# Gated recurrence: cumulated decays made two rounds ahead, and their logarithm moved to the begin of a round

## The chip, the cores and the metric

One NeuronCore of a Trainium2 chip runs the kernel; the other cores are idle. The metric is the time of one execution on the device in microseconds (us), lower is better. It is taken over several executions of the same compiled program, without the profiler.

## The reference, cut to what matters

The kernel computes two blocks, one behind the other, on 256 positions of 1024 channels, in fp32. The first block has a mixer with two branches (a gated linear recurrence, HGRN2, and a Mamba-2 recurrence) and a gated feed-forward net. The second has retention and a convolution as mixer, and 16 experts, each 1024 x 2048 twice and 2048 x 1024 once. The change touches only the HGRN2 branch, which has 8 heads of 128 channels and 272 positions (16 learned ones ahead of the 256):

```python
f = lb + (1.0 - lb) * jax.nn.sigmoid(f_pre)      # lb: one value for each channel
k = 1.0 - f
log_f = jnp.log(f)
bcum = jnp.cumsum(gc, axis=2)                    # gc: log_f in chunks
blast = bcum[:, :, -1]
q_dec = qc * jnp.exp(bcum)
k_inv = kc * jnp.exp(-bcum)
k_end = kc * jnp.exp(blast[:, :, None] - bcum)
...
o = o * lax.rsqrt(jnp.mean(o * o, axis=-1, keepdims=True) + EPS)
return (o * norm_w * jax.nn.silu(g))
```

## The kernel before

All engines run programs written out by hand, and they meet only at semaphores; an engine works through its own program strictly in the written order. Channels lie on the 128 partitions and positions along the free dimension, so one head of HGRN2 is one tile of 128 x 272.

The first block's input projection has 52 column tiles of 128 channels, j = 0 to 51. TensorE (PE) computes tile j (L872) and ScalarE (ACT) evicts it from one of three PSUM banks, with the activation that the column needs (evict, L1254). PE may open tile j only when tile j-3 has been evicted. The work of the recurrences is hung between these tiles: each engine's loop over j first does its share of the recurrences, then its share of the tile. From j = 32 on, head h of HGRN2 is worked on in round h, the three tiles j = 32+3h, 33+3h and 34+3h. What a round does, engine by engine:

- PE: in the first third `hg_turn(h)` (L784). It waits for `hg_staged` (the decayed queries and keys are ready), transposes values and keys (L793, L795), computes four levels of scores (L802), waits for `hg_v`, does one small score product (L804), waits for `hg_ke` and computes the state updates (L808). In the second third `hg_out(h)` (L815 to L818), which waits for `hg_masked`. In the last third `hg_mean(h)` (L826).
- VectorE (DVE): in the first third `hg_values(h)` (copies of the transposed values, L1845, L1846), `hg_mask(h)` (L1853, L1855), `hg_states(h)` (L1859, L1860), then `hg_cumulate(h+1)`; in the second third `hg_gate(h)` (L1867), `hg_finish(h-1)` (L1872) and `hg_decay(h+1)` (L1835 to L1840), whose end raises `hg_staged`.
- ACT: in the first third `hg_keys(h)` (L1373), `hg_log_mean(h-1)` (L1365), `hg_log(h+1)` (L1351), `hg_inverse(h-1)` (L1369); then it waits for the head's output, squares it (L1390) and does `hg_exps(h+1)` (L1356 to L1358); only then it evicts the tile.

`hg_cumulate(h)` is the step around which the change turns. It forms the gate f from the sigmoid in one DVE instruction (L1817, waited for), tells ACT (`hg_f`), forms k = 1 - f (L1819), waits for ACT's logarithm (`hg_log`), does four scans over chunks of 16, 32, 64 and 128 positions (L1822) and four differences (L1826), and raises `hg_b`:

```python
st.link(ts(hg_f, proj[:, h + TF_, :], oml[:, h:h + 1], lb[:, h:h + 1], ALU.mult, ALU.add))
dve.nop().then_inc(ev("hg_f"), 1)
st(ts(hg_k, hg_f, -1.0, 1.0, ALU.mult, ALU.add))
dve.wait_ge(ev("hg_log"), h + 1)
for l in range(4):
    st(dve.tensor_tensor_scan(hg_B[:, b, l, :], reset[:, l, :], hg_lf, 0.0, ALU.mult, ALU.add))
```

`hg_exps(h)` waits for `hg_b`, and `hg_decay(h)` for the exponentials (`hg_exp`). hg_B, hg_D and hg_K0 have two buffers, by h modulo 2; the logarithm hg_lf and the key factor hg_k have one each. Head 0 is prepared ahead of the rounds, at j = 30: behind the last output of Mamba-2 (`m2_out`, L1794) DVE clears two tiles (L1925, L1926) and calls `hg_cumulate(0)` and `hg_decay(0)`. Between the rounds stand two more pieces: the gating of Mamba-2's outputs on DVE (`m2_gate`, L1800, at j = 48 and behind the loop), whose squares ACT takes at j = 49 (L1400), and the modulation of the second block (L1668, L1717 on PE and DVE's L1672) in round 0.

The weights are streamed from HBM by one queue, SP's. Each transfer waits until PE has counted the slot of the ring free (`units_used`). In the second block's experts the same ring takes 2 MB units.

Of the kernel before, what the change touches and what calls it, by code (L numbers as in the profile page):

```python
# [19 lines left out]
ACT = mybir.ActivationFunctionType  # L20
ALU = mybir.AluOpType
# [11 lines left out]
HEADS = 8  # L33
# [15 lines left out]
TQ, TF_, TI, TG, TZ, TX, TBM, TCM = 0, 8, 16, 24, 32, 40, 48, 50  # L49
# [101 lines left out]
def build(nc, a, out):  # L151
    with ExitStack() as ctx:
# [5 lines left out]
        def ev(name):  # L158

            if name not in sems:  # L160
                sems[name] = ctx.enter_context(nc.semaphore("s_" + name))
            return sems[name]
# [30 lines left out]
        small = sb("small", [P, 256])  # L193
# [38 lines left out]
        proj = A.take(NPROJ, T)  # L232
# [24 lines left out]
        hg_S = A.take(2, P)  # L257
        hg_inv = A.take(1, T)[:, 0]

        hg_f, hg_k, hg_lf, hg_sq = (proj[:, TBM + i, :] for i in range(4))  # L260

        A = Arena(x_at)
        m2_t = A.take(2, T)
# [984 lines left out]
        def _(act):  # L1248
            st = Steps(act, ev("act_steps"))
# [97 lines left out]
                    act.activation(buf, buf, ACT.Exp).then_inc(ev("m2_seg_exp"), 1)  # L1347

            def hg_log(h):
                act.wait_ge(ev("hg_f"), h + 1)  # L1350
                act.activation(hg_lf, hg_f, ACT.Ln).then_inc(ev("hg_log"), 1)  # L1351

            def hg_exps(h):
                b = h % 2
                act.wait_ge(ev("hg_b"), h + 1)
                st(act.activation(hg_K0[:, b], hg_B[:, b, 0, :], ACT.Exp, scale=-1.0))  # L1356
                st.link(act.activation(hg_D[:, b], hg_D[:, b], ACT.Exp))
                act.activation(hg_B[:, b], hg_B[:, b], ACT.Exp).then_inc(ev("hg_exp"), 1)  # L1358
# [16 lines left out]
            def hgrn(j):  # L1375
                h = (j - 32) // 3
                if j < 32 or h >= HEADS:
                    return
                if (j - 32) % 3 == 0:
                    hg_keys(h)  # L1380
                    if h:
                        hg_log_mean(h - 1)
                    if h + 1 < HEADS:
                        hg_log(h + 1)
                    if h:
                        hg_inverse(h - 1)
                    act.wait_ge(ev("hg_out"), h + 1)
                    if h:
                        act.wait_ge(ev("hg_mean"), h)
                    act.activation(hg_sq, ps[:, 6, 0:T], ACT.Square).then_inc(ev("hg_squared"), 1)  # L1390
                    if h + 1 < HEADS:
                        hg_exps(h + 1)
                if (j - 32) % 3 == 2 and h == HEADS - 1:
                    hg_log_mean(h)
                    hg_inverse(h)
# [58 lines left out]
            for i in range(FT):  # L1454
                for s in range(2):
# [3 lines left out]
                    if i >= 2:  # L1459
                        act.wait_ge(ev("act_full"), i - 1)  # L1460
                    act.activation(fc[:, i % 2, s, :], bank_of(f"f{2 * i + s}")[:, 2:KEPT], ACT.Identity, scale=pc("ffw2", m),
                                   bias=pc("ffb", m)).then_inc(ev("ffn_tap"), 1)
# [140 lines left out]
        def _(dve):  # L1603
            st = Steps(dve, ev("dve_steps"))
            tt, ts, stt = dve.tensor_tensor, dve.tensor_scalar, dve.scalar_tensor_tensor
# [30 lines left out]
            st.link(dve.reciprocal(small[:, 24:32], small[:, 16:24]))  # L1636
            lb, oml = small[:, 96:104], small[:, 104:112]
            st.link(tt(lb, small[:, 0:8], small[:, 24:32], ALU.mult))
            st.link(ts(oml, lb, -1.0, 1.0, ALU.mult, ALU.add))

            def scaled(name, k, t0):
# [172 lines left out]
            def hg_cumulate(h):  # L1814
                b = h % 2
                dve.wait_ge(ev("proj_tiles"), 16 if h < 4 else 32)
                st.link(ts(hg_f, proj[:, h + TF_, :], oml[:, h:h + 1], lb[:, h:h + 1], ALU.mult, ALU.add))  # L1817
                dve.nop().then_inc(ev("hg_f"), 1)
                st(ts(hg_k, hg_f, -1.0, 1.0, ALU.mult, ALU.add))  # L1819
                dve.wait_ge(ev("hg_log"), h + 1)  # L1820
                for l in range(4):
                    st(dve.tensor_tensor_scan(hg_B[:, b, l, :], reset[:, l, :], hg_lf, 0.0, ALU.mult, ALU.add))  # L1822
                st.wait()
                for l, w in enumerate(LEVELS):
                    B = hg_B[:, b, l, 0:256].rearrange("p (c w) -> p c w", w=w)
                    st(tt(hg_D[:, b, l, :].rearrange("p (c w) -> p c w", w=w),  # L1826
                          B[:, :, w - 1:w].to_broadcast([P, 256 // w, w]), B, ALU.subtract))
                st.wait()
                dve.nop().then_inc(ev("hg_b"), 1)
# [44 lines left out]
            def hgrn(j):  # L1874
                h = (j - 32) // 3
                if j < 32 or h >= HEADS:
                    return
                if (j - 32) % 3 == 0:
                    hg_values(h)
                    hg_mask(h)  # L1880
                    hg_states(h)
                    if h == 0:
                        mod_add(1)
                    if h + 1 < HEADS:
                        hg_cumulate(h + 1)
                if (j - 32) % 3 == 1:
                    hg_gate(h)
                    if h:
                        hg_finish(h - 1)
                    if h + 1 < HEADS:  # L1890
                        hg_decay(h + 1)
                if (j - 32) % 3 == 2 and h == HEADS - 1:
                    hg_finish(h)

# [387 lines left out]
```

## Time and profile before

| | us |
|---|---|
| median of 3 executions | 1703.27 |
| lowest, highest | 1703.02, 1706.29 |
| the profiled execution, its own time | 1704.49 |
| its span in the trace | 1702.7 |

| engine | busy us | share of the span |
|---|---|---|
| PE (matmul) | 1349.4 | 79% |
| DVE | 507.1 | 30% |
| ACT | 450.4 | 26% |
| POOL | 232.8 | 14% |

PE is TensorE, DVE VectorE, ACT ScalarE, POOL GpSimd, SP the sync engine, whose queue issues the loads. A line of the timeline has the start in us, the duration of the group in us, the engine, the source line, the operation, and in brackets how long the engine had been idle before it and what released it. "PEclk" is the clock that TensorE was granted, as a share of 2.4 GHz; 0.50 is its lower level of 1.2 GHz. The rounds of HGRN2 lie between about 187 and 327 us of the span.

### The profile page before, as it was taken

Reading aid. Unit: us, or ns where it says so; the run is one execution under the profiler, and the core shown is the slowest. Engines: PE = TensorE matmul, PEld = TensorE weight load, DVE = VectorE, ACT = ScalarE, POOL = GpSimd, SP = SyncE. Lnnn points to the kernel's source line nnn. Section 1 sums busy time; section 2 is a strip of 40 time slices with the busy share of each in tenths; the row PEclk is TensorE's granted clock in tenths of the full one; section 3 lists DMA queues with packets and bytes.
Section 4 is the critical chain, followed back from the end, with each engine's and each line's share of the span. In section 5 each row is a group of like instructions: output and inputs, shape, how many; then the busy total and the mean of one; then the engine's idle time right before and its main releaser. Section 6 shows DMA issues by size and latency. Waiting matters only on the chain.

```text
span 1702.7 us, 21054 instructions
## 1 busy us (share of the span) xinstructions
PE 1349.4 (79%) x8581; PEld 831.1 (49%) x8581; DVE 507.1 (30%) x919; ACT 450.4 (26%) x675; POOL 232.8 (14%) x100
## 2 busy tenths in 40 slices
PE   6989999999999999988767577666657667666665
PEld 4877788879998988944222122112212221221221
DVE  3874677436568455622000000000000000000001
ACT  4853465436564533721000000000000000000001
POOL 0000000028767654400000000000000000000000
PEclk9999999999999999997887878888887877987887
DMA  7936322168534552285999999999999999999995
GB/s 242 361 149 235 112 99 100 50 210 273 186 137 181 201 188 99 100 357 212 428 429 428 429 428 429 428 428 429 429 429 428 429 429 428 429 428 429 428 428 250
DMA packets 92335, 524.01 MB, mean 308 GB/s; under 512 B 8009, under 2 KB 30945, under 8 KB 64369
## 3 DMA queue, kind: packets, MB, share of 16 engines
q1 hardware_dynamic: 92057, 523.08, 75.4%
q8 instruction: 44, 0.72, 0.2%
q14 instruction: 18, 0.15, 0.0%
q10 hardware_dynamic: 216, 0.06, 0.0%
HBM read 522.08 MB, written 1.05 MB: 307 GB/s over the span
## 4 chain that ended last, share of the span: by engine, by line
DMA 47%; PE 38%; DVE 8%; ACT 3%; issue 1%; SPq 1%; POOL 0%; ACTq 0%; DVEq 0%
DMA ring<-in_w_down 23%; DMA ring<-in_w_up 23%; PE ps L657 6%; PE ps L661 6%; PE ps L658 6%; PE ps L1213 3%; PE ps L890 3%; PE ps L1226 3%; PE ps L872 2%; PE ps L1123 2%; PE ps L641 1%; SPq L502 1%; DVE arena L2024 1%; PE ps L802 1%; PE ps L706 1%
## 5 line engine op out<-in xcount | busy, mean ns | idle before, releaser
L1213 PE MATMUL ps<-ring,arena 128*32 128x512 f32 x1984 | 297.5, 745 | 163.2 <-DMA ring<-in_w_up 136.0
L1599 POOL TENSOR_TENSOR ring_r<-ring,ring_r 128x1024 fp32r<-128x1024 f32 (+1 forms) x96 | 232.6, 2441 | 483.3 <-ACT ring_r L1265 483.3
L657 PE MATMUL ps<-arena_r,ring_r 128*128 128x258 f32 (+3 forms) x960 | 289.3, 301 | 9.7 <-PE ps L661 3.4
L661 PE MATMUL ps<-arena_r,ring_r 128*128 128x258 f32 (+3 forms) x960 | 281.4, 293 | 0.0
L1226 PE MATMUL ps<-ring,arena 128*32 128x512 f32 x1024 | 171.2, 804 | 104.1 <-DMA ring<-in_w_down 97.1
L1213 PEld LDWEIGHTS ps<-ring,arena 128*32 128x32 f32 x1984 | 65.0, 127 | 378.3 <-DMA ring<-in_w_up 204.7
L657 PEld LDWEIGHTS ps<-arena_r,ring_r 128*128 128x128 f32 x960 | 183.2, 191 | 20.6 <-issue 13.2
L661 PEld LDWEIGHTS ps<-arena_r,ring_r 128*128 128x128 f32 x960 | 182.4, 190 | 2.9
L658 PE MATMUL ps<-arena_r,ring_r 128*128 128x256 f32 (+2 forms) x608 | 180.8, 297 | 0.0
L2239 DVE TENSOR_TENSOR arena<-arena,ps 128x512 f32<-128x512 f32 x16 | 11.0, 688 | 448.7 <-PE ps L1213 448.7
L1226 PEld LDWEIGHTS ps<-ring,arena 128*32 128x32 f32 x1024 | 33.0, 129 | 225.1 <-DMA ring<-in_w_down 147.6
L1265 ACT ACTIVATE ring_r<-ring 128x1024 fp32r<-128x1024 f32 (+1 forms) x122 | 126.0, 1037 | 42.9 <-PE ps L658 23.0
L658 PEld LDWEIGHTS ps<-arena_r,ring_r 128*128 128x128 f32 x608 | 116.3, 191 | 4.0 <-issue 1.0
L872 PE MATMUL ps<-uT,ring 128*128 128x272 f32 x416 | 100.2, 395 | 3.2 <-DVE uT L1643 3.2
L658 PE MATMUL ps<-uT_r,ring_r 128*128 128x258 f32 x352 | 99.5, 283 | 0.0
L2241 DVE COPY arena<-ps 128x512 f32<-128x512 f32 x16 | 11.1, 692 | 290.7 <-PE ps L1226 290.7
L1569 ACT ACTIVATE arena<-ps 128x512 f32<-128x512 f32 x16 | 9.6, 597 | 316.1 <-PE ps L1218 316.1
L872 PEld LDWEIGHTS ps<-uT,ring 128*128 128x128 f32 x416 | 77.6, 190 | 18.5 <-issue 3.6
L1567 ACT ACTIVATE arena<-ps 128x512 f32<-128x512 f32 x16 | 9.6, 597 | 282.7 <-PE ps L1213 282.7
L1573 ACT ACTIVATE arena<-ps 128x512 f32<-128x512 f32 x16 | 9.6, 597 | 264.6 <-PE ps L1226 264.6
L1235 PE MATMUL ps<-arena 128*128 128x512 f32 x128 | 67.1, 672 | 14.2 <-DVEq L2248 13.5
L641 PEld LDWEIGHTS ps<-arena,hT 128*128 128x128 f32 x512 | 65.8, 205 | 8.9 <-issue 7.1
(370 smaller groups left out, 1478.1 us busy)
## 6 DMA issues: line engine op xcount, KB each, us to landing
ring<-in_w_gate SPq DMA_DIRECT2D x64, 2048.0 KB, 25.9
ring<-in_w_down SPq DMA_DIRECT2D x64, 2048.0 KB, 26.2
ring<-in_w_up SPq DMA_DIRECT2D x60, 2048.0 KB, 21.9
ring<-in_w_in SPq DMA_DIRECT2D x20, 2048.0 KB, 11.7
ring<-in_w_ada SPq DMA_DIRECT2D x12, 2048.0 KB, 8.5
ring<-in_ffn_w_up SPq DMA_DIRECT2D x22, 1024.0 KB, 7.9
ring<-in_w_out SPq DMA_DIRECT2D x6, 2048.0 KB, 8.0
ring<-in_ffn_w_down SPq DMA_DIRECT2D x4, 2048.0 KB, 8.4
```

Of the source, the lines that this page charges most:

```text
L641: mm = pe.matmul(o, l, r, start=i == 0, stop=i == len(pairs) - 1)
L657: pe.matmul(o, hi[:, k, :], r_(xhi(k0 + k)), start=first and k == 0, stop=False)
L658: mm = pe.matmul(o, hi[:, k, :], r_(xlo(k0 + k)), start=False, stop=False)
L661: mm = pe.matmul(o, lo[:, k, :], r_(xhi(k0 + k)), start=False, stop=last and k == nk - 1)
L872: mm = pe.matmul(o[:, 0:T], w[:, k, :], uT[:, k, :], start=k == 0, stop=k == KT - 1)
L890: mm = pe.matmul(o[:, 0:KEPT], kcols(u_out[cb][half], m)[:, i, :], x, start=first and n == 0, stop=last and n == len(blocks) - 1)
L1123: mm = pe.matmul(ps[:, 4 + 2 * w + cb, :], x[:, w * P:w * P + P], slot(u_out2[cb]).rearrange("p (k c) -> p k c", k=KT)[:, i, :], start=n = ...
L1213: mm = pe.matmul(ps[32 * j:32 * j + 32, half, :], xs[:, kt, :], wk[:, 512 * j:512 * j + 512], start=kt == 0, stop=kt == KT - 1)
L1226: mm = pe.matmul(ps[32 * j:32 * j + 32, half, :], heT[:, j, 32 * i:32 * i + 32], w[:, j, 512 * half:512 * half + 512], start=i == 0, stop= ...
L1235: mm = pe.matmul(ps[:, 4 + b, :], Gt[:, w * P:w * P + P], ye[:, half * 512:half * 512 + 512], start=first, stop=last, skip_group_check=True)
L1265: act.activation(r_(rounded(c)), chunks[c][1], ACT.Copy).then_inc(ev("w_hi"), 1)
L1599: pool.tensor_tensor(r_(w), w, f_(rounded(c)), ALU.subtract).then_inc(ev("w_lo"), 1)
```

## The change

The gate f is no longer written by DVE. ACT takes the logarithm straight from the sigmoid, ln(oml x sigmoid + lb), with oml = 1 - lb and lb as scale and bias of each partition. DVE forms the key factor in one instruction, (lb - 1) x sigmoid + oml, for which a small tile noml = lb - 1 is made once at the start. `hg_log(h)` waits for `hg_b` of the head before (the scans there must have read hg_lf), and for head 0 for the last output of Mamba-2.

The order in the rounds changes. In round h from 1 on, DVE does `hg_decay(h+1)` directly behind `hg_states(h)`, and `hg_cumulate(h+2)` behind gate and finish. ACT does `hg_log(h+2)` behind `hg_log_mean(h-1)` and `hg_exps(h+1)` ahead of the wait for the head's output. In round 0, DVE does `hg_cumulate(1)` behind the states as before, and behind the gate first `hg_decay(1)` and then `hg_cumulate(2)`; ACT does `hg_log(1)` behind the keys, and `hg_exps(1)` and `hg_log(2)` behind the square.

```diff
             def hg_log(h):
-                act.wait_ge(ev("hg_f"), h + 1)
-                act.activation(hg_lf, hg_f, ACT.Ln).then_inc(ev("hg_log"), 1)
+                if h:
+                    act.wait_ge(ev("hg_b"), h)
+                else:
+                    act.wait_ge(ev("m2_out"), 8)
+                lb, oml = small[:, 96 + h:97 + h], small[:, 104 + h:105 + h]
+                act.activation(hg_lf, proj[:, h + TF_, :], ACT.Ln, scale=oml, bias=lb).then_inc(ev("hg_log"), 1)
...
                     hg_keys(h)
                     if h:
                         hg_log_mean(h - 1)
-                    if h + 1 < HEADS:
-                        hg_log(h + 1)
+                    else:
+                        hg_log(1)
+                    if h and h + 2 < HEADS:
+                        hg_log(h + 2)
+                    if h and h + 1 < HEADS:
+                        hg_exps(h + 1)
                     if h:
                         hg_inverse(h - 1)
                     act.wait_ge(ev("hg_out"), h + 1)
                     if h:
                         act.wait_ge(ev("hg_mean"), h)
                     act.activation(hg_sq, ps[:, 6, 0:T], ACT.Square).then_inc(ev("hg_squared"), 1)
-                    if h + 1 < HEADS:
-                        hg_exps(h + 1)
+                    if h == 0:
+                        hg_exps(1)
+                        hg_log(2)
...
+            noml = small[:, 112:120]
+            st(ts(noml, lb, -1.0, None, ALU.add))
...
-                st.link(ts(hg_f, proj[:, h + TF_, :], oml[:, h:h + 1], lb[:, h:h + 1], ALU.mult, ALU.add))
-                dve.nop().then_inc(ev("hg_f"), 1)
-                st(ts(hg_k, hg_f, -1.0, 1.0, ALU.mult, ALU.add))
+                st(ts(hg_k, proj[:, h + TF_, :], noml[:, h:h + 1], oml[:, h:h + 1], ALU.mult, ALU.add))
...
-                    if h + 1 < HEADS:
-                        hg_cumulate(h + 1)
+                    if h == 0:
+                        hg_cumulate(1)
+                    elif h + 1 < HEADS:
+                        hg_decay(h + 1)
                 if (j - 32) % 3 == 1:
                     hg_gate(h)
                     if h:
                         hg_finish(h - 1)
-                    if h + 1 < HEADS:
-                        hg_decay(h + 1)
+                    else:
+                        hg_decay(1)
+                    if h + 2 < HEADS:
+                        hg_cumulate(h + 2)
```

## Rows read from the trace of the kernel before

**Rows 1.** Busy time by stretch; granted clock, DMA share and GB/s come last

```profile
800.00:1702.70 902.70, 601.83 (x3666) 192.72 (x3658) 51.08 (x117) 50.34 (x69) 0.00 (x0) 0.82 0.99 420
...
170.00:340.00 170.00, 164.49 (x888) 137.01 (x886) 107.71 (x224) 89.70 (x131) 0.00 (x0) 0.99 0.25 91
```

**Rows 2.** Chain that ended last, behind 811 us: start us, us, what

```profile
811.49 21.37 DMA ring<-in_w_up
...
835.02 27.20 DMA ring<-in_w_down
```

**Rows 3.** PE's timeline, rounds 0 and 1

```profile
187.67 0.55 PE L793 MATMUL ps<-cst,arena 128*128 128x128 f32 x3 [2.12 <-DVEq L1841]
...
206.95 0.55 PE L793 MATMUL ps<-cst,arena 128*128 128x128 f32 x3 [0.65 <-DVEq L1841]
...
209.43 0.21 PE L804 MATMUL ps<-arena 128*16 128x16 f32 x2
```

**Rows 4.** PE's timeline, rounds 5 and 6

```profile
272.77 0.55 PE L793 MATMUL ps<-cst,arena 128*128 128x128 f32 x3 [0.20 <-DVEq L1841]
...
289.20 0.51 PE L793 MATMUL ps<-cst,arena 128*128 128x128 f32 x3
...
292.82 0.71 PE L808 MATMUL ps<-arena 128*128 128x128 f32 x4 [0.96 <-ACT arena L1373]
```

**Rows 5.** Busy time, granted clock last but two, behind the wait at 186 us

```profile
189.00:192.00 3.00, 3.00 (x16) 2.74 (x15) 0.32 (x2) 1.16 (x1) 0.00 (x0) 0.50 1.05 399
```

**Rows 6.** PE's idle times elsewhere, and the clock behind the second

```profile
96.97 1.50 PE L735 MATMUL ps<-cst,arena 128*128 128x128 f32 x12 [2.04 <-DVEq L1736]
...
121.72 1.47 PE L760 MATMUL ps<-arena_r 48*128 48x128 f32 x12 [1.67 <-DVE arena L1794]
...
124.00:127.00 3.00, 3.00 (x15) 3.00 (x15) 2.86 (x8) 1.41 (x3) 0.00 (x0) 0.50 0.00 0
```

**Rows 7.** DVE's timeline, head 0

```profile
175.99 0.50 DVE L1794 SCALAR_TENSOR_TENSOR arena<-arena,bcast,ps 128x272 f32<-128x272 f32 x1 [0.65 <-PE ps L781]
...
176.94 0.42 DVE L1817 TENSOR_SCALAR arena<-arena,small 128x272 f32<-128x272 f32 x1
...
177.91 2.57 DVE L1822 TENSOR_TENSOR_SCAN arena<-cst,arena 128x272 f32<-128x272 f32 x4
180.52 1.43 DVE L1826 TENSOR_TENSOR arena<-arena 128x256 f32<-128x256 f32 x4
```

**Rows 8.** ACT line with scale and bias of each partition: ns, min/median/max

```profile
L1430 ACT ACTIVATE arena<-arena,par x12: 612/616/618, 31.0 to 70.4; 128x272 f32<-128x272 f32 x12
```

**Rows 9.** DVE's timeline, begin of round 1

```profile
207.75 0.42 DVE L1845 COPY arena<-ps 128x256 f32<-128x256 f32 x1 [0.92 <-PE ps L795]
208.10 0.27 DVE L1846 COPY arena<-ps 16x128 f32<-16x128 f32 x1
```

**Rows 10.** DVE's timeline, round 5 (its first tile starts at 272.77)

```profile
277.95 0.35 DVE L1860 SCALAR_TENSOR_TENSOR arena<-arena,small,ps 128x128 f32<-128x128 f32 x1
...
283.68 0.50 DVE L1867 SCALAR_TENSOR_TENSOR arena<-ps,par,arena 128x272 f32<-128x272 f32 x1 [0.22 <-DVE arena L1826]
284.10 0.43 DVE L1872 TENSOR_TENSOR arena<-arena 128x272 f32<-128x272 f32 x1
286.10 0.15 DVE L1835 COPY small<-arena 128x1 f32<-128x1 f32 x1 [1.57 <-ACT arena L1358]
...
289.27 1.29 DVE L1800 TENSOR_TENSOR arena<-arena 128x1088 f32<-128x1088 f32 x1 [0.21 <-DVE arena L1840]
```

**Rows 11.** ACT's timeline, round 5

```profile
273.98 1.28 ACT L1365 ACT_TABLE_LOAD   x1
275.27 0.49 ACT L1365 ACTIVATE arena<-ps,eps 128x272 f32<-128x272 f32 x1
...
281.52 0.40 ACT L1390 ACTIVATE arena<-ps 128x272 f32<-128x272 f32 x1 [0.39 <-PE ps L818]
283.55 0.43 ACT L1356 ACTIVATE arena<-arena 128x272 f32<-128x272 f32 x1 [1.63 <-DVEq L1829]
```

More of the change, by code:

```diff
@@ L258, in build @@
         hg_inv = A.take(1, T)[:, 0]
-        hg_f, hg_k, hg_lf, hg_sq = (proj[:, TBM + i, :] for i in range(4))
+        hg_k, hg_lf, hg_sq = (proj[:, TBM + i, :] for i in range(1, 4))
         A = Arena(x_at)
```

## The prediction

> **What bounds the kernel now.** I read the busy times by stretch first, then the chain that ended last, then the timelines of the rounds. From 800 us to the end the DMA engines are busy 99% and move 420 GB/s, while in the stretch of the rounds, 170 to 340 us, they are at 25% and PE is busy for 164.5 of 170 us [rows 1]. The chain shows the same: behind 811 us it is made of loads of the experts' weights, 27.2 us each [rows 2], and before that of PE. SP's queue waits for PE's `units_used` until then, so I let a microsecond won or lost by PE in the rounds move the stream of the experts, and with it the end, by one microsecond.
>
> So this stretch can give back at most PE's idle time in it, 170.00 - 164.49 = 5.5 us, plus what the clock costs. The reader should see in PE's timeline where that idle time lies. Two waits are for `hg_staged`: 2.12 us ahead of round 0 and 0.65 us ahead of round 1 [rows 3]. One of 0.20 us stands ahead of round 5, and 0.96 us in round 6 are spent in wait for ACT's copy of the keys [rows 4]. The rest is pieces of 0.3 us or less, mostly PE waiting for its own last tile. In most rounds PE is the bound already, and an earlier `hg_staged` brings nothing there.
>
> The clock matters as much. Behind the wait of 2.12 us TensorE runs at 0.50, its lower level of 1.2 GHz, for over 3 us [rows 5]; 3 us at half speed lose 1.5 us, with the edges of the stretch 1.6. Elsewhere an idle time of 1.67 us was followed by the lower level too, one of 2.04 us was not [rows 6]. I read from this that an idle time of 1.5 to 3 us is a toss-up which costs 1.6 us when it goes wrong.
>
> **The change part by part.** *Head 0.* Now the last output of Mamba-2 ends at 175.99 + 0.50 = 176.49, the gate starts at 176.94 and the scans at 177.91 [rows 7]. The gate's instruction is replaced by the key factor of the same form and 0.42 us, and the scans stand directly behind it, at 176.94 + 0.42 = 177.36. The logarithm must be there by then. It is started by the output at 176.49. Ln with scale and bias of each partition is not in the trace; the nearest rows are the same Ln without them, 0.43, and an Identity with both, 0.62 [rows 8]. Even with 0.62 it ends at 177.1, ahead of 177.36. Gain 177.91 - 177.36 = 0.55 us, bounds 0.4 and 0.6. All of it comes off the wait of 2.12 us, of which some 1.6 us are left.
>
> *Round 0.* `hg_cumulate(1)` is still on the path to `hg_staged(1)` and loses the same two steps, 0.55 us, which comes off the 0.65 us ahead of round 1 [rows 3]. ACT's added `hg_log(2)` behind `hg_exps(1)` costs a table load of 1.28 us, 0.6 us for Ln and puts the evictions of tiles 32 and 33 off by 1.9 us. The cover is the three banks: PE wants the first of them back for tile 35, over 3 us behind the turn at 206.95. Nothing.
>
> *Round 1, the loss.* `hg_cumulate(2)` now stands behind `hg_decay(1)` and ahead of `hg_values(1)`. `hg_decay(1)` ends exactly where PE starts the turn of round 1, since PE waits for it. DVE then needs 0.42 (key factor) + 2.57 (scans) + 1.43 (differences) [rows 7] + 0.2 (last one waited for) = 4.6 us until it turns to the values, and 0.62 us for these (0.35 from the first copy's start to the second's, and 0.27) [rows 9]; with 0.1 for the two signals 5.3 us. PE stands at L804 and waits for `hg_v` after 209.43 - 206.95 = 2.48 us [rows 3]. It is held 5.3 - 2.5 = **2.8 us**, bounds 2.5 and 3.1. Behind L804 wait L808, tile 35 and everything else on PE.
>
> *Does this come back each round?* Take round 5, from 272.77. DVE ends the states at 278.30, 5.5 us in. ACT ends the mean's logarithm at 275.76, 3.0 in [rows 10, 11]. New order: Ln 0.62, table load 1.28, the three exponentials 286.10 - 283.55 = 2.55, from their start to DVE's release [rows 10, 11], so they end 7.45 us in. The decay takes 289.06 - 286.10 = 2.96, to 10.4; gate and finish 0.85, to 11.3 [rows 10]; the cumulate 4.6, to 15.9. The next round starts 289.20 - 272.77 = 16.43 us after this one [rows 4] and PE stands at L804 only 2.5 us later. With 0.7 for the values DVE has until 18.2 us in, so 2.3 us are to spare. Rounds 2 to 7 are not held. In them `hg_staged` comes 6 us early, the square is not late (the exponentials and the inverse are over before 8 us, and the output comes at 281.52, 8.7 us in [rows 11]), and the evictions follow it without exponentials in between. What goes is the wait ahead of round 5, 0.20 us and a weight load that was late with it: 0.3 us, bounds 0 and 0.5.
>
> *Round 6.* Mamba-2's gating now ends 15.9 + 0.2 + 1.29 = 17.4 us into round 5, which is 1.0 us into round 6; now it ends at 290.56, 1.4 us in [rows 4, 10]. ACT's squares, then the tile, then the keys follow it, so the 0.96 us at L808 lose 0.4, bounds 0 and 0.96.
>
> *The clock.* The idle time of 2.8 us in round 1 is longer than either of those behind which the clock fell. I add 1.6 us, bounds 0 and 1.7. The wait ahead of round 0, then about 1.6 us, I let cost what it does now, bounds 0 and a gain of 1.6. [...]
>
> *The rest.* The small tile noml is one DVE instruction near 22 us, hidden while DVE waits for ACT. The end of the rounds is bound by PE's own products and moves with the rest. No transfer changes.
>
> **Sum:** -0.55 - 0.55 - 0.3 - 0.4 + 2.8 + 1.6 = **+2.6 us**. The profiled execution took 1704.49 (span 1702.7), so a profiled one of the changed kernel would take 1707.1. The median shown is 1703.27, 1.2 lower, so I forecast a median of 1705.9. Differences under 0.2%, 3.4 us, can't be told from none by a measurement of this kernel.
>
> **The rivals.** *The clock falls only once:* it holds behind the new stall, or behind the shortened wait ahead of round 0 while it falls in round 1. Then the sum is +1.0, a time of 1704.3; with no fall at all it is -0.6, 1702.7. For it: 2.04 us went by without a fall. Against: the longer time. Chance 0.37 for the two together.
>
> *DVE's new order holds PE in every round (slower).* The place is L804 of rounds 2 to 6, the condition that the cumulate ends more than 18.2 us into the round before, 2.3 us behind my 15.9. Each microsecond beyond costs 5 rounds x 1 us. It takes exponentials 2.3 us later than 7.45, for instance by a second table load between Ln and the exponentials and slower signals. At 3 us later it is 5 x 0.7 = 3.5 us on top: 1709.4. Against: every term comes from a row. Chance 0.12.
>
> *No stall (faster).* If `hg_values(1)` were not held, through a cumulate that is far shorter than its rows or values that PE needs late, only the gains remain: -1.8, and -3.4 with the clock held ahead of round 0: 1699.9. The order in the code speaks against it. Chance 0.06.
>
> *The change does nothing it says:* the two steps out of the cumulate could be hidden behind ACT's logarithm if this started later than I have it. Then 0.55 + 0.55 us more: 1707.0. Chance 0.05.
>
> **How the numbers follow.** The forecast has 0.40. Its bounds together run from 1703.27 - 0.4 - 0.6 - 0.5 - 0.96 + 2.5 - 1.6 = 1701.7 to 1703.27 - 0.4 - 0.4 + 3.1 + 1.7 = 1707.3. Executions scatter by up to 3 us upwards, so the range is 1701.4 to 1708.6. Over 0.2% slower, beyond 1706.7: the slower rival, half of the last one, and some of the forecast's upper part, 0.21. Faster, below 1699.9: 0.07. Within: 0.72.
>
> **What would show it.** In round 1 L804 idle for some 2.8 us released by L1846, and in no other round; the wait ahead of round 0 at 1.6 us, ahead of round 1 at 0.1; DVE's scans directly behind the key factor; the granted clock at 0.50 for 3 us in round 1. The forecast is wrong if L804 never waits there (then the kernel is faster), if it waits in each round (slower), or if PE reaches the experts earlier or later and the end doesn't follow.

## The result, and the time and profile after

| us | before | after |
|---|---|---|
| median | 1703.12 (6 executions) | 1711.46 (6 executions) |
| lowest, highest | 1702.71, 1706.29 | 1706.12, 1714.61 |
| the profiled execution, its own time | 1704.49 | 1706.12 |
| its span | 1702.7 | 1704.3 |

The ratio is 1.0041, with a 95% interval of 1.0029 to 1.0053. The forecast was 1705.9, the range 1701.4 to 1708.6, so the prediction was wrong: the kernel is slower by 0.4%, some 8 us by the medians. The profiled execution was the fastest of the six. Its trace therefore shows what the change does to the order of the work, but less than the median loss.

The page of the changed kernel, its span and busy times, and below it the busy time by stretch (columns as in [rows 1]):

```profile
span 1704.3 us, 21040 instructions
...
PE 1356.5 (80%) x8581; PEld 831.2 (49%) x8581; DVE 509.3 (30%) x912; ACT 451.9 (27%) x676; POOL 232.1 (14%) x100
```

```profile
170.00:340.00 170.00, 164.03 (x895) 137.19 (x894) 105.82 (x221) 92.10 (x133) 0.00 (x0) 1.00 0.27 96
189.00:192.00 3.00, 3.00 (x26) 2.83 (x27) 1.58 (x4) 2.19 (x3) 0.00 (x0) 1.00 1.05 404
212.00:215.00 3.00, 3.00 (x15) 2.52 (x15) 2.20 (x7) 2.96 (x5) 0.00 (x0) 1.00 0.00 0
800.00:1704.30 904.30, 612.89 (x3702) 194.97 (x3694) 51.16 (x117) 50.32 (x69) 0.00 (x0) 0.81 0.99 421
```

The last stretch is bound by the stream of weights as before, 0.99 busy at 421 GB/s. The clock behind the wait ahead of round 0 is at 1.00 now, where it was at 0.50 [rows 5], and it is at 1.00 behind the new stall too.

PE's timeline, rounds 0 and 1, against [rows 3], then rounds 5 and 6, against [rows 4]:

```profile
188.98 0.55 PE L793 MATMUL ps<-cst,arena 128*128 128x128 f32 x3 [1.47 <-DVEq L1850]
...
206.09 0.55 PE L793 MATMUL ps<-cst,arena 128*128 128x128 f32 x3
...
211.35 0.21 PE L804 MATMUL ps<-arena 128*16 128x16 f32 x2 [2.72 <-DVEq L1857]
...
274.31 0.49 PE L793 MATMUL ps<-cst,arena 128*128 128x128 f32 x3
...
290.68 0.49 PE L793 MATMUL ps<-cst,arena 128*128 128x128 f32 x3
...
293.74 0.71 PE L808 MATMUL ps<-arena 128*128 128x128 f32 x4 [0.41 <-ACT arena L1377]
```

The wait ahead of round 0 is 1.47 us (2.12 before), that ahead of round 1 is gone, and PE stands for 2.72 us at L804 in round 1. No other round has such a stall. DVE's timeline in round 1 shows what PE waits for, against [rows 9]:

```profile
206.12 0.42 DVE L1828 TENSOR_SCALAR arena<-arena,small 128x272 f32<-128x272 f32 x1
206.46 2.56 DVE L1831 TENSOR_TENSOR_SCAN arena<-cst,arena 128x272 f32<-128x272 f32 x4
209.06 1.43 DVE L1835 TENSOR_TENSOR arena<-arena 128x256 f32<-128x256 f32 x4
210.63 0.42 DVE L1854 COPY arena<-ps 128x256 f32<-128x256 f32 x1
210.97 0.27 DVE L1855 COPY arena<-ps 16x128 f32<-16x128 f32 x1
```

The scans stand directly behind the key factor, and the whole cumulate of head 2 runs while the transposed values wait to be copied: 210.63 - 206.09 = 4.5 us, then 0.6 for the values.

So far the prediction holds. What it lacked lies 260 and 500 us behind the stall, in parts that the change doesn't touch. The table has PE's time from one landmark to the next: the first transposes of rounds 0, 1 and 2 (L793); the first sum of squares of Mamba-2's gated outputs (L672, in round 6); the feed-forward net's first product (L657); a wait of 1.16 us for POOL among the products of its second matrix (at 541.87 us before); and the first product of the second block's output projection (L1123), which stands ahead of the router. `after_again` is a second profile of the changed kernel; `after_less` is an experiment told below.

| stretch, us of PE | before | after | after_again | after_less |
|---|---|---|---|---|
| round 0 to round 1 | 19.28 | 17.10 | 17.11 | 17.09 |
| round 1 to round 2 | 16.43 | 19.22 | 22.23 | 19.22 |
| round 2 to the sum of squares (L672) | 79.74 | 78.73 | 78.71 | 78.66 |
| from there to the feed-forward net | 71.39 | 71.40 | 71.40 | 71.39 |
| feed-forward net, to the wait for POOL | 167.36 | 169.47 | 169.48 | 167.35 |
| from there to the output projection (L1123) | 186.26 | 186.59 | 188.14 | 184.80 |

The feed-forward stage, as this stretch is called from here on, is 2.1 us longer in the changed kernel. The last stretch holds the end of the feed-forward net, the second block's input projection (the q tiles) and the retention. Before, it held 3.4 us at the lower clock from 550.4 us on, which cost 1.5; `after` did not have these, so it also has 1.8 us more than it ought to: 186.59 - (186.26 - 1.47) = 1.80.

**The feed-forward stage.** DVE and POOL before, then DVE, POOL and PE after:

```profile
464.52 0.43 DVE L1987 TENSOR_TENSOR arena<-arena 128x256 f32<-128x256 f32 x1 [0.25 <-DVE arena L1983]
464.87 0.42 DVE L1975 TENSOR_TENSOR arena_r<-arena,arena_r 128x256 fp32r<-128x256 f32 x1
...
464.97 4.94 POOL L1599 TENSOR_TENSOR ring_r<-ring,ring_r 128x1024 fp32r<-128x1024 f32 x2 [4.46 <-ACT ring_r L1265]
```

```profile
464.14 0.48 DVE L1995 SCALAR_TENSOR_TENSOR arena<-ps,par,arena 128x256 f32<-128x256 f32 x1 [0.60 <-DVE arena L1996]
464.66 0.48 DVE L1996 SCALAR_TENSOR_TENSOR arena<-ps,par,arena 128x256 f32<-128x256 f32 x1
465.39 0.43 DVE L2000 TENSOR_TENSOR arena<-arena 128x256 f32<-128x256 f32 x1 [0.25 <-DVE arena L1996]
465.74 2.62 DVE L1988 TENSOR_TENSOR arena_r<-arena,arena_r 128x256 fp32r<-128x256 f32 x1
...
465.49 5.11 POOL L1608 TENSOR_TENSOR ring_r<-ring,ring_r 128x1024 fp32r<-128x1024 f32 x2 [4.26 <-ACT ring_r L1265]
...
471.65 0.38 PE L657 MATMUL ps<-arena_r,ring_r 128*128 128x258 f32 x1 [1.50 <-DVEq L1997]
```

The same subtraction, L1975 then and L1988 now, takes 0.42 us where it starts 0.1 us ahead of POOL's operation, and 2.62 us where it starts 0.25 us behind it: it ends 0.3 us behind the first of POOL's two. PE waits for its result. DVE is late because it pauses: ahead of L1995 stand 0.60 us of idle time, where the same step elsewhere has 0.25. In fifteen of the sixteen traces a pause of 0.35 us stands ahead of the DVE instruction with number 703 (counted from 0, signals included). In the kernel before, that is the step at 455.30 us, and PE then waits 0.66 us at 463.14 instead of some 0.25, a small cost. The changed kernel has 15 DVE instructions fewer ahead of it (each of eight heads saves a signal and a TENSOR_SCALAR, and noml adds one), so the pause meets a step 15 instructions further on, at 464.14 us, and this makes the collision.

**The retention.** ACT, DVE and POOL before, then with PE after:

```profile
712.07 0.42 ACT L1509 ACTIVATE cst<-arena 128x256 f32<-128x256 f32 x1 [0.39 <-ACT arena L1254]
...
713.35 0.69 DVE L2087 TENSOR_TENSOR arena<-arena,cst 128x512 f32<-128x512 f32 x1
...
713.51 2.79 POOL L1599 TENSOR_TENSOR ring_r<-ring,ring_r 128x1024 fp32r<-128x1024 f32 x1 [0.98 <-ACT ring_r L1265]
```

```profile
713.35 0.42 ACT L1518 ACTIVATE cst<-arena 128x256 f32<-128x256 f32 x1
...
714.91 2.81 DVE L2100 TENSOR_TENSOR arena<-arena,cst 128x512 f32<-128x512 f32 x1
...
714.79 2.38 POOL L1608 TENSOR_TENSOR ring_r<-ring,ring_r 128x1024 fp32r<-128x1024 f32 x1 [0.70 <-ACT ring_r L1265]
...
719.25 0.96 PE L1091 MATMUL ps<-cst,hT 128*128 128x128 f32 x7 [1.89 <-DVEq L2108]
```

It is the same collision with the other sign. Before, ACT pauses for some 0.3 us ahead of its instruction with number 831 (counted from 0), which is L1509: it was idle for 0.39 us there and for 0.11 in the changed kernel. This holds POOL's next operation back until DVE's has begun. The changed kernel has one ACT instruction more (1035 for 1034, a table load), the pause no longer stands there, POOL comes 0.1 us ahead of DVE, and DVE's 0.69 us become 2.81.

### The profile page after: what moved, and what is told of

It is laid out like the page before. It is cut to its first block, busy times and chain, and to the rows that moved or that the text cites. A ratio compares the mean times of both kernels' runs of the same rounds, so it can differ in the third digit from the quotient of the medians.

```text
span 1704.3 us, 21040 instructions
## 1 busy us (share of the span) xinstructions
PE 1356.5 (80%) x8581; PEld 831.2 (49%) x8581; DVE 509.3 (30%) x912; ACT 451.9 (27%) x676; POOL 232.1 (14%) x100
## 4 chain that ended last, share of the span: by engine, by line
DMA 46%; PE 40%; DVE 8%; ACT 3%; issue 1%; POOL 0%; SPq 0%; DVEq 0%; ACTq 0%
DMA ring<-in_w_down 23%; DMA ring<-in_w_up 23%; PE ps L657 6%; PE ps L661 5%; PE ps L658 5%; PE ps L872 4%; PE ps L1213 3%; PE ps L890 3%; PE ps L1226 3%; PE ps L1123 2%; PE ps L641 1%; PE ps L706 1%; DVE arena L2037 1%; DVE arena L1831 1%; ACT ring_r L1265 1%
## 5 line engine op out<-in xcount | busy, mean ns | idle before, releaser
L1213 PE MATMUL ps<-ring,arena 128*32 128x512 f32 x1984 | 298.6, 748 | 158.2 <-DMA ring<-in_w_up 132.4
L657 PE MATMUL ps<-arena_r,ring_r 128*128 128x258 f32 (+3 forms) x960 | 288.9, 301 | 10.2 <-PE ps L661 3.4
L1226 PE MATMUL ps<-ring,arena 128*32 128x512 f32 x1024 | 178.7, 835 | 99.0 <-DMA ring<-in_w_down 91.5
L657 PEld LDWEIGHTS ps<-arena_r,ring_r 128*128 128x128 f32 x960 | 182.8, 190 | 21.3 <-issue 13.4
L1235 PE MATMUL ps<-arena 128*128 128x512 f32 x128 | 63.2, 639 | 14.2 <-DVEq L2261 13.5
```

What stands on the lines that cost most here:

```text
L657: pe.matmul(o, hi[:, k, :], r_(xhi(k0 + k)), start=first and k == 0, stop=False)
L1213: mm = pe.matmul(ps[32 * j:32 * j + 32, half, :], xs[:, kt, :], wk[:, 512 * j:512 * j + 512], start=kt == 0, stop=kt == KT - 1)
L1226: mm = pe.matmul(ps[32 * j:32 * j + 32, half, :], heT[:, j, 32 * i:32 * i + 32], w[:, j, 512 * half:512 * half + 512], start=i == 0, stop= ...
L1235: mm = pe.matmul(ps[:, 4 + b, :], Gt[:, w * P:w * P + P], ye[:, half * 512:half * 512 + 512], start=first, stop=last, skip_group_check=True)
```

## The experiments

Ratios are to the kernel before on the same chip, with 95% intervals. Theory A of a run is always the one that I held when I wrote it down.

### The changed kernel once more

No edit.

> The changed kernel again, unchanged. Theory A (the wait of 2.72 us in round 1, and on top of it which stretches of a run fall to 1.2 GHz): the idle times of TensorE stay what they were, and its clock falls at other places than in the first trace, so executions scatter over some 8 us and the median is 1708 to 1712. Theory B (a fixed cost that the first trace missed by chance): the median is 1711 again and this trace shows some 5 us more at one place.

Measured: 1710.56 us, ratio 1.0052 (1.0036 to 1.0069). The stall is 2.72 us again, and this time the clock fell with it (granted clock last but two):

```profile
209.00:212.00 3.00, 2.56 (x10) 2.17 (x11) 2.45 (x8) 2.94 (x4) 0.00 (x0) 0.50 0.00 0
212.00:215.00 3.00, 3.00 (x8) 2.30 (x7) 2.29 (x6) 1.43 (x2) 0.00 (x0) 0.50 0.00 0
```

The lower level lasted 6.8 us in all and cost 22.23 - 19.22 = 3.0 us, twice what I had put down. Both waits behind the rounds are there again.

### The fold alone, without the new order

```diff
-                act.wait_ge(ev("hg_f"), h + 1)
-                act.activation(hg_lf, hg_f, ACT.Ln).then_inc(ev("hg_log"), 1)
+                if h:
+                    act.wait_ge(ev("hg_b"), h)
+                else:
+                    act.wait_ge(ev("m2_out"), 8)
+                lb, oml = small[:, 96 + h:97 + h], small[:, 104 + h:105 + h]
+                act.activation(hg_lf, proj[:, h + TF_, :], ACT.Ln, scale=oml, bias=lb).then_inc(ev("hg_log"), 1)
...
+            noml = small[:, 112:120]
+            st(ts(noml, lb, -1.0, None, ALU.add))
...
-                st.link(ts(hg_f, proj[:, h + TF_, :], oml[:, h:h + 1], lb[:, h:h + 1], ALU.mult, ALU.add))
-                dve.nop().then_inc(ev("hg_f"), 1)
-                st(ts(hg_k, hg_f, -1.0, 1.0, ALU.mult, ALU.add))
+                st(ts(hg_k, proj[:, h + TF_, :], noml[:, h:h + 1], oml[:, h:h + 1], ALU.mult, ALU.add))
```

> The kernel of before with the logarithm taken straight from the sigmoid and the key factor in one instruction, all steps where they stood. Theory A (the order makes the loss, the folded gate gains): waits ahead of rounds 0 and 1 shorter by 0.5 us each, no wait at the small score product of round 1, a time of 1702.0 (1700.5 to 1703.5). Theory B (any shift of this part lands the clock's falls otherwise and costs the 8 us): 1706 or more.

Measured: **1699.37 us**, ratio 0.9982 (0.9969 to 0.9995). Rounds 0 to 1 take 17.11 us and rounds 1 to 2 take 16.43: both gains ahead of the rounds, no stall. Round 2 to the sum of squares (L672) takes 78.67, as in the changed kernel: the wait ahead of round 5 is gone here too, and that in round 6 is down to 0.34 us.

```profile
290.44 0.71 PE L808 MATMUL ps<-arena 128*128 128x128 f32 x4 [0.34 <-ACT arena L1377]
```

The new order therefore brings nothing in the rounds that the fold alone doesn't; it costs the stall. The wait of the feed-forward stage is there, that of the retention is not (this kernel has ACT's 1034 instructions):

```profile
462.47 2.62 DVE L1979 TENSOR_TENSOR arena_r<-arena,arena_r 128x256 fp32r<-128x256 f32 x1
...
468.38 0.39 PE L657 MATMUL ps<-arena_r,ring_r 128*128 128x258 f32 x1 [1.51 <-DVEq L1988]
```

### The stall alone, put into the kernel before

```diff
+                    if h == 1:
+                        for n in (4, 3):
+                            for l in range(n):
+                                st(dve.tensor_tensor_scan(hg_B[:, 0, l, :], reset[:, l, :], hg_lf, 0.0, ALU.mult, ALU.add))
+                            st.wait()
                     hg_values(h)
```

> The kernel of before, and seven scans more on VectorE ahead of the values of round 1, whose results are written over later. They hold TensorE at the small score product of round 1 for about 2.6 us, as the changed order does. Theory A (the stall alone, and the clock with it, makes the loss): 1706 to 1711, scattered as the changed kernel. Theory B (the loss comes from the order of the later rounds): 1705.7, as tight as before.

Measured: 1708.97 us, ratio 1.0035 (1.0022 to 1.0048).

```profile
216.65 0.24 PE L804 MATMUL ps<-arena 128*16 128x16 f32 x2 [2.79 <-DVEq L1848]
```

Seven scans hold PE for 2.79 us. Round 1 to 2 took 20.81 us, 4.4 more than before: the stall and one fall of the clock. The median is 5.6 us higher, so a stall of 2.8 us costs more than its own length. Neither of the two later waits appears (feed-forward stage 167.02 us, last stretch 186.26): a shift in time alone does not bring them. This kernel has 8 DVE instructions more than the kernel before, and its number 703 waits 1.43 us for ACT in any case, so that no pause shows there; the feed-forward stage is 0.34 us shorter than before.

### The cumulate of head 2 behind the values

```diff
                     hg_values(h)
+                    if h == 1:
+                        hg_cumulate(2)
...
-                    if h + 2 < HEADS:
+                    if h and h + 2 < HEADS:
                         hg_cumulate(h + 2)
```

> The changed kernel with the cumulate of head 2 behind the values of round 1 and not ahead of them. The wait of 2.72 us at the small score product goes, and one of some 1.9 us takes its place at the head's output, which waits for the masks. Theory A: the waits come to 0.8 us less, so 1 us under the changed kernel, within the scatter of the clock. Theory B (that the values are late is the whole loss): 1703 or less.

Measured: 1707.46 us, ratio 1.0025 (1.001 to 1.004). The stall moved instead of going:

```profile
216.08 0.63 PE L815 MATMUL ps<-arena 128*128 128x128 f32 x2 [1.96 <-DVEq L1870]
```

L804 is free, but now the masks stand behind the cumulate, PE waits 1.96 us for them, and the clock fell there too, for 6.8 us. The order in round 1 matters, but both places tried, ahead of the values and ahead of the masks, are too early.

### Bare nops on DVE and ACT

```diff
+                for _ in range(2 if h else 1):
+                    dve.nop()
                 dve.wait_ge(ev("hg_log"), h + 1)
```

Two of these kernels had this edit, one on the fold alone and one on the changed kernel; the third is the fold alone with one `act.nop()` ahead of `hg_log(0)`.

> The kernel with the folded gate alone, and 15 empty instructions on VectorE in the cumulates (two for each head, one for head 0), so that every later instruction of VectorE has the number in its program that it had before. Theory A (a pause of 0.35 us sits at a fixed place in VectorE's program, the 703rd instruction of its trace, and in the folded kernels it pushes a subtraction of the feed-forward net behind one of GpSimd's, 2.1 us): the pause is back at 455 us, where it is harmless, the feed-forward stage is 2.1 us shorter than in the folded kernel, time 1697.3 (1696 to 1699). Theory B (the 2.1 us come from where the stage starts in time): the same as the folded kernel, 1699.4.

> The kernel with the folded gate alone, and one empty instruction on ScalarE at tile 30, so that its later instructions have the numbers of the changed kernel. Theory A (the second loss of the changed kernel, a wait of 1.89 us in the retention stage, comes from the one instruction more on ScalarE, the added table load, which takes a pause of 0.35 us away from the square there and lets GpSimd start ahead of VectorE): the wait of 1.89 us appears here too, time 1.8 us above the folded kernel, 1701.2. Theory B (the wait comes from the order in the rounds or from the time at which the stage starts): no such wait, 1699.4.

> The changed kernel and the 15 empty instructions on VectorE. Theory A: the 2.1 us in the feed-forward net go, the wait of 2.72 us in round 1 and the 1.89 us in the retention stage stay, time 2.1 us below the changed kernel, 1708.5 to 1709.5. Theory B: as the changed kernel, 1710.5 to 1711.5.

Measured: 1701.50 us, 0.9986 (0.9973 to 0.9999); 1701.40, 0.9987 (0.9975 to 0.9998); 1708.95, 1.0033 (1.0021 to 1.0046). The nops without a signal left no instruction in the trace: the counts stay (DVE 1389 in `fold_pad` and `after_pad`, ACT 1034 in `fold_act`), the pauses stay at the same steps, and the waits stay as they were. The three tell nothing about the theories; they serve as repeats of kernels already run, and agree with them within their intervals. In the profiled execution of the last one the clock held behind the stall.

### PE kept busy in the stall

```diff
+                if h == 1:
+                    pe.wait_ge(ev("tiles_freed"), opened[0] - TB + 1)
+                    for _ in range(6):
+                        pe.matmul(bank_of("p35")[:, 0:T], ones1[:], uT[:, 0, :], start=True, stop=True)
                 pe.wait_ge(ev("hg_v"), h + 1)
```

> The changed kernel and six products of 128 x 272 on TensorE ahead of its wait in round 1, 2.7 us of work whose result is written over. Theory A (behind the wait the clock falls in most executions, for 3.4 or 6.8 us): TensorE waits for under 0.2 us there, goes on at the same moment as in the changed kernel, and never falls to 1.2 GHz in round 1, so the median comes down by about 2 us, to 1709. Theory B (the clock has no share in it): 1711.

Measured: 1709.73 us, ratio 1.0036 (1.0024 to 1.0049). The products that nobody reads fill the stall:

```profile
206.89 2.92 PE L806 MATMUL ps<-uT,ones 128*128 128x272 f32 x12
209.77 0.22 PE L808 MATMUL ps<-arena 128*16 128x16 f32 x2
```

The clock stays at 1.00 from 207 to 213 us in the one execution that was traced. The median is no lower than the 1708.95 us of the changed kernel with bare nops on the same chip. So a fall right behind the stall is not what makes the kernel slow as a whole; with intervals of 2 us to either side, a share of 1 us, which five falls in eight would have, can't be excluded. The stall itself, the later waits and falls elsewhere remain.

### The DVE count put back, with signals

Signals that nobody waits for do count: with 15 of them DVE has 1404 instructions in the trace for 1389. They stand ahead of head 0, where DVE is idle.

```diff
+                if j == 30:
+                    for _ in range(15):
+                        dve.nop().then_inc(ev("pad"), 1)
```

> The kernel with the folded gate alone, and 15 signals that nobody waits for on VectorE ahead of its wait at tile 30, where it has 3 us of idle time; in the trace they count as instructions, which the empty ones without a signal did not. Theory A (a pause of 0.35 us at the 703rd instruction of VectorE's trace): the pause is back behind the same instruction as in the kernel of before, some 9 us earlier in the feed-forward net than in the folded kernel, the stage from the feed-forward's begin to the retention's is 2.1 us shorter, and the median is 2 us under the folded kernel's, 1697 to 1699. Theory B (the 2.1 us have another cause): the stage stays as long as in the folded kernel.

> The changed kernel and the 15 signals on VectorE. Theory A: the 2.1 us in the feed-forward net go, the waits of 2.72 us in round 1 and of 1.89 us in the retention stage stay; median 2 us under the changed kernel's, 1708 to 1709.5. Theory B: the stage stays as long as in the changed kernel, 1710 to 1711.5.

Measured: on the fold alone **1699.61 us**, ratio 0.9974 (0.9964 to 0.9984), with all nine executions between 1698.07 and 1700.39; on the changed kernel 1709.19, 1.0031 (1.0021 to 1.0041). In both the pause is back at the step where it was, and the feed-forward stage takes 167.36 and 167.43 us. In the stage the 2.1 us are gone by nothing but 15 instructions without effect. The medians don't tell this apart: the ratios are 0.0008 under the fold alone and 0.001 under the changed kernel, and the intervals overlap. In the changed kernel the stall and the wait of the retention stay.

### One ACT instruction more

```diff
                 if j == 30:
+                    act.nop().then_inc(ev("pad"), 1)
                     hg_log(0)
```

> The kernel with the folded gate alone, and one signal that nobody waits for on ScalarE at tile 30, so that its later instructions have the numbers of the changed kernel. Theory A (the wait of 1.89 us in the retention stage comes from the number of ScalarE's instructions): the wait appears, 1.8 us more in that stage, and the median is 1701 to 1703. Theory B (it comes from the order in the rounds): no such wait.

Measured: 1704.69 us, ratio 1.0010 (0.9997 to 1.0022). On the same chip this is 5.1 us above the fold with 15 DVE signals, which has neither wait; the two waits explain 3.9. The expected range ended at 1703.

```profile
712.68 2.81 DVE L2092 TENSOR_TENSOR arena<-arena,cst 128x512 f32<-128x512 f32 x1
...
717.01 1.06 PE L1091 MATMUL ps<-cst,hT 128*128 128x128 f32 x8 [1.89 <-DVEq L2100]
```

One signal on ACT, some 535 us earlier, brings the wait of the retention into a kernel that did not have it.

### 64 ACT instructions more, and one fewer

703 and 831 are both one below a multiple of 64. From these two numbers alone I estimated that the pause comes back every 64 instructions. The first kernel adds 63 signals on ACT to the one with the 15 on DVE, ahead of `hg_log_mean(7)` (the expectation below names head 2, where they do not stand). The second instead takes one ACT signal out of it, at the start of the program:

```diff
-            st(act.activation(cond[:, :, 0], pc("c", 0, 8), ACT.Silu))
-            st.link(act.activation(cond[:, :, 1], pc("cctx", 0, 8), ACT.Silu))
-            act.nop().then_inc(ev("cond_ready"), 1)
+            st.link(act.activation(cond[:, :, 0], pc("c", 0, 8), ACT.Silu))
+            act.activation(cond[:, :, 1], pc("cctx", 0, 8), ACT.Silu).then_inc(ev("cond_ready"), 1)
```

The third is the one with the 15 signals again, on the same chip as the second.

> The kernel with 15 signals on VectorE (as before) and in addition 63 signals on ScalarE ahead of the log of head 2's mean, in 6.5 us in which ScalarE has nothing to do, so that ScalarE's instructions of the retention carry numbers that are 64 higher than in the kernel before. [...] Theory B (the pause is tied to the number 831 alone, or the wait has another source): the wait of 1.89 us at L1091 stays, median about 1709.2. [...]

> The kernel with 15 signals on VectorE, in which ScalarE in addition gives one signal fewer at its very begin (the second Silu of the conditioning raises it itself), so that ScalarE's instructions of the retention carry the numbers that they have in the kernel before. The 64 signals more of the run before did not bring the pause of 0.35 us back to its old instruction; one fewer must, if the number of instructions counts at all and only the assumed period was wrong. Theory A (ScalarE's number decides about the wait at L1091): the pause stands at instruction 831 again, ahead of ret_square, the wait of 1.89 us at L1091 goes, the stretch from the q tiles to L1123 is 1.8 us shorter than with the 15 signals alone; median 1.8 us, or a ratio of 0.001, under that kernel on the same chip. Theory B (the wait at L1091 comes from something else that the changed kernel does): it stays, and the two medians agree within 0.5 us.

> The kernel with 15 signals on VectorE once more, on the same chip as the one with a signal fewer on ScalarE, as the measure for it. It had 1709.2 us and a ratio of 1.0031. Theory A and theory B: a ratio of 1.003 again, the wait of 1.89 us at L1091 there, none of 2.1 us in the feed-forward stage. If it comes out at the 1.0012 of the kernel with 64 signals on ScalarE, then the difference between those two was scatter between executions and chips, and not an effect of the signals.

Measured: 63 more 1705.43 us, ratio 1.0012 (1.0000 to 1.0025); one fewer **1703.43**, 1.0001 (0.9988 to 1.0013); the repeat 1705.10, 1.0006 (0.9994 to 1.0017). ACT, DVE and PE of the kernel with one signal fewer, then PE of the repeat and of the one with 63 more:

```profile
711.36 0.42 ACT L1517 ACTIVATE cst<-arena 128x256 f32<-128x256 f32 x1 [0.39 <-ACT arena L1254]
...
712.65 0.69 DVE L2102 TENSOR_TENSOR arena<-arena,cst 128x512 f32<-128x512 f32 x1
...
715.21 1.04 PE L1091 MATMUL ps<-cst,hT 128*128 128x128 f32 x8
```

```profile
723.69 1.06 PE L1091 MATMUL ps<-cst,hT 128*128 128x128 f32 x8 [1.89 <-DVEq L2111]
```

```profile
719.45 1.06 PE L1091 MATMUL ps<-cst,hT 128*128 128x128 f32 x8 [1.87 <-DVEq L2113]
```

The estimate of 64 fell: with 63 more the pause did not return to that step (ACT was idle for 0.12 us ahead of it, at number 895) and the wait stayed, 1.87 us. With one fewer it did return, 0.39 us ahead of number 831, and the wait went. In these runs the instruction number decides. Whether and when the pause comes back no run shows; the traces have one more such place, DVE's number 1087, where a step takes 0.47 us in the kernels with 1404 DVE instructions and the same step, then number 1072, 0.10 in those with 1389. 703, 831 and 1087 lie 128 and 256 apart, but no run tested 128. The 63 signals took 0.07 us each and cost PE nothing: the stretch in which they stand, from L672 to the feed-forward net, takes 71.40 us as before. What the expectation of one fewer calls the stretch from the q tiles is the last one of the table. One fewer is 1.7 us under the repeat, for 1.8 expected, though the intervals overlap.

The repeat also tells how far to trust a median: the same kernel had a ratio of 1.0031 on one chip and 1.0006 on another, intervals that don't meet. Each run was taken on one chip, so it can't be told whether the chip or the occasion makes the difference.

## Why the prediction was wrong

**Right in size, in the rounds.** From the table and the timelines: the stall 2.72 us (2.8 forecast), in round 1 alone; the wait ahead of round 0 shorter by 2.12 - 1.47 = 0.65 (0.55); that ahead of round 1 gone, 0.65 (0.55); round 5 0.35 (0.3); round 6 0.41 left of 0.96 (0.55 for 0.4). Without the clock the steps sum to +1.0 in the forecast. Measured, they are -0.65 - 0.65 + 2.79 (round 1 to 2) - 1.01 (round 2 to L672) = +0.5. The cause of the last term was not the forecast one. I put the gains in rounds 5 and 6 down to the new order, `hg_staged` 6 us earlier; the fold alone, with the old order, has them in full (78.67 for 78.73 us). A slip in the sum of the lower bound takes one of the two gains of 0.55 us at 0.4, where 0.6 is its bound; it moves the bound by 0.2 us.

**The clock, mis-sized, with both signs.** The forecast had 1.6 us for one fall behind the stall, none gained. Behind the stall of 2.7 to 2.8 us the clock fell in five of eight profiled executions (not in `after`, `after_pad` and `after_less`), for 3.4 us in four of them and for 6.8 in one; it cost 1.5 to 1.7 us, or 3.0, and 1.2 on the average of the eight. Ahead of round 0, where I had left the cost as it was, it never fell behind 1.47 us, in any profile of a kernel with the fold: of the 2.18 us that round 0 to 1 lost, 1.53 are this. With this gain the clock at these two places costs next to nothing in sum, where I had +1.6.

**The step that failed** is a term put at nothing without a reason, that of the stages behind the rounds. The prediction let each microsecond of the rounds reach the experts unchanged, and under "The rest" it put nothing for the stages in between. They don't keep their length. The change takes 15 instructions from DVE and gives one to ACT, and a pause of 0.3 to 0.35 us that is tied to the number of the instruction meets other steps: +2.1 us in the feed-forward stage and +1.8 in the retention. Both are shown in the stage times, each put in or taken out by instructions that compute nothing (`fold_num`, `after_num`, `fold_act1`, `after_less`). No rival had this mechanism. With both counts as before, the changed kernel is level with the kernel before, 1.0001 (0.9988 to 1.0013), which agrees with the +0.5 us of the rounds. In its profiled execution PE reaches L1123 at 727.42 us, 0.7 ahead of before. This is close to the -0.6 of my rival in which the clock never falls, but by luck: both executions have three falls, at different places.

**What is left.** The measured steps come to 0.5 + 2.1 + 1.8 = +4.4 us. The medians differ by 8.3 and, in the three further kernels that are or act as the changed one, by 5.7 to 7.2. The cause of the remaining 1 to 4 us is open. More falls of the clock elsewhere are not shown: ahead of 750 us the eight profiles with the stall had 10.2 to 27.3 us at the lower level, the seven with neither this stall nor the one of `values_first` 3.4 to 20.5, the kernel before 10.2. What is left also does not belong to the kernel alone. Over the +2.3 us that its stall and retention wait account for, the kernel with 15 signals was left with 4.0 us on one chip (`after_num`) and 0.5 below it on another (`after_num2`).

The assumption that what PE loses reaches the stream of the experts holds: in `after` PE is 3.4 us late at L1123, and the last packet of weights lands 3.7 us later, at 1687.69 for 1684.02. That the span is only 1.6 us longer comes from what stands behind this packet, which took 16.6 us for 18.7, where the last products ran at a granted clock of 1.00 (from 1692.25 to 1696 us); before, it was 0.59 (from 1688.85 to 1695 us). Before, then after:

```profile
1688.85 6.20 PE L1235 MATMUL ps<-arena 128*128 128x512 f32 x8 [0.72 <-ACT arena L1573]
```

```profile
1692.25 3.70 PE L1235 MATMUL ps<-arena 128*128 128x512 f32 x8 [0.69 <-ACT arena L1582]
```

In all profiles this last piece takes 15.2 to 18.7 us, so it alone scatters a time by 3.5 us, and one pair of profiles can't be compared by its spans.

**A version that beats both** is the fold alone with the old order, 0.9982, and 0.9986 and 0.9987 in its two repeats. With 15 signals for the pause it had 0.9974, which these intervals don't tell from the rest.

## What to carry to other kernels

Split such a change: the fold (one instruction and a signal fewer on the path) was the gain, the reorder only moved a 4.5 us step ahead of something that PE needs at once. Here 15 instructions fewer on DVE cost 2.1 us, and one more on ACT 1.8 us, in stages that the edit never touches, so compare stage by stage, and, to judge the edit by itself, put the count of instructions back with signals that nobody waits for. The same kernel had a ratio of 1.0031 on one chip and 1.0006 on another, some 4 us in 1700, so differences of this size need more than one chip, or more than one occasion, to be told apart.

## What the hardware did that I had not expected

- A pause at a fixed instruction number, 0.35 us at DVE's 703 and 0.28 at ACT's 831 (counted from 0); adding or taking away instructions that compute nothing moves it to another step. Signals count (15 of them, DVE 1404 for 1389 instructions), bare nops don't (1389 with and without). 63 more on ACT did not bring it back to its step.
- The DVE TENSOR_TENSOR that started 0.25 us behind one of POOL's in the feed-forward stage was held until 0.3 us behind that one's end, and so was the one that started 0.1 us behind in the retention (until 0.5 us behind): 0.42 us became 2.62, and 0.69 became 2.81. Started 0.10 and 0.16 us ahead of POOL's, they took the 0.42 and 0.69. In the sixteen traces all 79 of the 128x256 ones that write fp32r (2.39 to 2.63 us each) and all 73 of 128x512 (2.20 to 2.82) that started while POOL worked were held, and 192 of the 259 plain 128x256 ones (1.07 to 2.63; the others took 0.42 to 0.55); what spared the others is open.
- TensorE's clock went either way behind the same wait. The stall of 2.7 us went by with and without a fall, and the single one of 1.96 us brought one of 6.8 us. The wait of 2.04 us at L735, behind which the clock held in the trace of before, came with a fall in nine of the sixteen traces, the shorter one of 1.67 us at L760 in all sixteen. Waits of 1.47 to 1.49 us never brought one ahead of round 0 (14 traces), but such waits at L1123, of 1.45 to 1.48 us, did in four of the sixteen (`after_again`, `after_pad`, `values_first`, `fold_act1`). So the length of the wait alone does not decide in these traces. At any time the granted clock in them is 1.00 or 0.50 (a value between is the mean of a window); they give it as a share alone, and what these levels are in GHz no run shows.
